# A third seven-product chunk in each wide round, with two weight sums made by adding DMAs

## The reference

```python
h = h + 0.5 * swiglu(rmsnorm(h, ffn1_norm[l]), ffn1_w_in[l], ffn1_w_out[l])   # w_in 2048 x 11264, w_out 5632 x 2048
u = rmsnorm(h, mix_norm[l]) @ w_in_mix[l]
...                                                                            # pooling and gated linear attention
h = h + 0.5 * swiglu(rmsnorm(h, ffn2_norm[l]), ffn2_w_in[l], ffn2_w_out[l])
...                                                                            # sparse attention, stick-breaking attention
```

## Time and profile before

| | before |
|---|---|
| median of 3 runs | 2668.81 us (2668.37 to 2668.97) |
| the profiled execution: time | 2668.85 us |
| the profiled execution: span of the trace | 2667.1 us |
| matmuls | 12038 |
| DMA traffic | 550.9 MB, mean 207 GB/s |

### The profile page before, as it was taken

The page is one execution under the profiler, slowest core; times in us unless marked ns, Lnnn a source line. Parts: engine busy times, 40 slices in busy tenths (PEclk is TensorE's granted clock), DMA queues, the critical chain, the costliest instruction groups (busy, mean ns, idle before and its releaser), DMA issues.

```text
span 2667.1 us, 32619 instructions
## 1 busy us (share of the span) xinstructions
PE 2655.7 (100%) x12038; PEld 2193.6 (82%) x12038; DVE 1926.6 (72%) x2464; ACT 1392.4 (52%) x1836; POOL 58.2 (2%) x64
## 2 busy tenths in 40 slices
PE   9999999999999999999999999999999999999999
PEld 7888888888888788888888888887888888888887
DVE  6888889886645466888888886758555576566566
ACT  6555555454544445555555454555554464675463
POOL 0000000000000000000000000030000000020000
PEclk9999999999999999999999999999999999999999
DMA  9767677677845466666576667755467576546754
GB/s 303 232 198 236 194 231 222 205 222 240 257 144 174 146 219 211 212 225 224 181 246 204 222 213 226 253 186 158 137 186 258 166 237 211 174 143 206 240 181 135
DMA packets 348575, 550.89 MB, mean 207 GB/s; under 512 B 40992, under 2 KB 120096, under 8 KB 347648
## 3 DMA queue, kind: packets, MB, share of 16 engines
q1 hardware_dynamic: 346624, 539.90, 63.4%
q0 software_dynamic: 1648, 8.86, 1.0%
q10 hardware_dynamic: 144, 0.04, 0.0%
HBM read 525.59 MB, written 23.07 MB: 206 GB/s over the span
## 4 chain that ended last, share of the span: by engine, by line
PE 98%; DMA 1%; SPq 0%; DVE 0%; ACT 0%; issue 0%; ACTq 0%; DVEq 0%
PE bank L1467 17%; PE bank L1469 17%; PE bank L1468 17%; PE bank L1536 14%; PE bank L1535 14%; PE bank L1534 14%; DMA raw<-in_ffn_w_in_dram 1%; PE bank L1426 1%; PE bank L1134 0%; PE bank L886 0%; PE bank L870 0%; PE bank L1114 0%; PE bank L568 0%; PE bank L840 0%; SPq L1315 0%
## 5 line engine op out<-in xcount | busy, mean ns | idle before, releaser
L1965 DVE TENSOR_TENSOR wlo<-raw,whi 128x1024 fp32r<-128x1024 f32 (+3 forms) x559 | 641.9, 1158 | 542.8 <-ACT whi L1616 537.8
L1616 ACT CAST whi<-raw 128x1024 fp32r<-128x1024 f32 (+3 forms) x559 | 548.9, 990 | 649.5 <-PE bank L1469 623.8
L1756 ACT CAST whi<-raw 128x1024 fp32r<-128x1024 f32 (+1 forms) x416 | 409.2, 998 | 413.3 <-PE bank L1536 405.8
L2125 DVE TENSOR_TENSOR wlo<-raw,whi 128x1024 fp32r<-128x1024 f32 (+1 forms) x416 | 463.3, 1150 | 67.3 <-ACT whi L1756 64.9
L1467 PE MATMUL bank<-whi,p_hi 128*128 128x512 f32 x1184 | 465.6, 393 | 3.1 <-DVE wlo L1965 3.1
L1469 PE MATMUL bank<-whi,p_lo 128*128 128x512 f32 x1184 | 461.1, 389 | 0.0
L1468 PE MATMUL bank<-wlo,p_hi 128*128 128x512 f32 x1184 | 460.9, 389 | 0.0
L1467 PE MATMUL bank<-whi,q_hi 128*128 128x512 f32 x864 | 340.6, 394 | 0.5 <-DVE wlo L1965 0.5
L1469 PE MATMUL bank<-whi,q_lo 128*128 128x512 f32 x864 | 336.6, 390 | 0.0
L1468 PE MATMUL bank<-wlo,q_hi 128*128 128x512 f32 x864 | 336.3, 389 | 0.0
L1467 PEld LDWEIGHTS bank<-whi,p_hi 128*128 128x128 f32 x1184 | 222.4, 188 | 52.7 <-issue 5.7
(11 more groups left out here) (381 smaller groups left out, 2984.6 us busy)
## 6 DMA issues: line engine op xcount, KB each, us to landing
raw<-in_ffn_w_in_dram SPq DMA_DIRECT2D x704, 256.0 KB, 3.8
raw<-in_ffn_w_out_dram SPq DMA_DIRECT2D x320, 256.0 KB, 4.0
raw<-in_w_in_a_dram SPq DMA_DIRECT2D x192, 256.0 KB, 3.1
raw<-in_w_in_mix_dram SPq DMA_DIRECT2D x128, 256.0 KB, 3.2
raw<-in_w_ple_gate_dram SPq DMA_DIRECT2D x128, 256.0 KB, 3.7
raw<-in_w_in_b_dram SPq DMA_DIRECT2D x128, 256.0 KB, 3.1
raw<-in_w_out_mix_dram SPq DMA_DIRECT2D x64, 256.0 KB, 3.3
raw<-in_w_o_a_dram SPq DMA_DIRECT2D x64, 256.0 KB, 3.7
```

Of the source, the lines that this page charges most:

```text
L1616: act.copy(whi[:, c % SPLIT, 0:n, 0:w], raw[:, c, 0:n, 0:w]).then_inc(hi_done, 1)
L1756: act.copy(whi[:, i % SPLIT, 0:n, :], raw[:, i % CH, 0:n, :]).then_inc(hi_done, 1)
L1965: dve.tensor_tensor(wlo[:, c % SPLIT, 0:n, 0:w], raw[:, c, 0:n, 0:w], whi[:, c % SPLIT, 0:n, 0:w].bitcast(F32), ALU.subtract).then_inc(lo_ ...
L2125: dve.tensor_tensor(wlo[:, i % SPLIT, 0:n, :], raw[:, i % CH, 0:n, :], whi[:, i % SPLIT, 0:n, :].bitcast(F32), ALU.subtract).then_inc(lo_d ...
```

## The change

`SEVEN` becomes (1, 3, 5). The first two weight sums of a chunk are made by a ScalarE copy of two blocks into `w_sums` (`weight_blocks`) and by two DMAs of GpSimd that add the third block, read again from HBM (`add_blocks`). VectorE makes only the other two sums. The order by hand is changed around this, and the buffers of operand sums hold three sets. The DMA descriptor scratch is set to 8192. The core of the diff:

```diff
-SEVEN = (2, 5)
+SEVEN = (1, 3, 5)
...
 SP, load and load_wide, behind the wait for lo_done:
+                        if unit_at(s, wide, i) - CH in summed_units:
+                            sp.wait_ge(t24_sum, summed_units[unit_at(s, wide, i) - CH] + 1)
...
 GpSimd, called for ffn1 after the constants are loaded and for ffn2 after the mixer's:
+            def add_blocks(tag):
...
+                    for i, c in enumerate(SEVEN):
+                        pool.wait_ge(sem("t13_blocks"), seven_number(s, wide, i) + 1)
...
+                        for m in range(2):
+                            pool.dma_start(w_sums[:, m, :], b12, accum_op=ALU.add).then_inc(t13_sum, 16)
...
 ScalarE:
-                for j in range(2):
-                    ins = act.copy(pair_hi[s.hid_pair][:, k * 2 + j, :].rearrange("p (t q n) -> p t q n", t=TT, q=4),
-                                   hidf[:, u, :, j, :, :].rearrange("p q t n -> p t q n"))
-                ins.then_inc(hid_hi, 1)
+                act.copy(pair_hi[s.hid_pair][:, k * 2:k * 2 + 2, :].rearrange("p j (t q n) -> p (j t) q n", t=TT, q=4),
+                         hidf[:, u, :, :, :, :].rearrange("p q j t n -> p (j t) q n")).then_inc(hid_hi, 1)
...
+            def weight_blocks(s, wide, c):
+                q = seven_number(s, wide, SEVEN.index(c))
+                if q:
+                    act.wait_ge(t13_used, q)
+                a_ = 2 * c % CH
+                for n in range(2):
+                    act.wait_ge(landed[a_ + n], (s.r0 + 2 * wide + 2 * c // CH) * 32 + 32)
+                act.copy(w_sums[:, 0:2, :], raw[:, a_:a_ + 2, 0, :]).then_inc(sem("t13_blocks"), 1)
...
             def begin_wide(s, wide, before):
+                weight_blocks(s, wide, SEVEN[0])
                 for i in range(3):
                     wide_hi(s, wide, i)
...
             def wide_round(s, wide):
+                sums_13_hi(s, wide, SEVEN[0])
+                sums_24_hi(s, wide, SEVEN[0])
                 for c in range(2, CH):
                     wide_hi(s, wide, 2 * c)
+                    if c - 1 in SEVEN[1:]:
+                        sums_13_hi(s, wide, c - 1)
+                        sums_24_hi(s, wide, c - 1)
...
                     wide_hi(s, wide, 2 * c + 1)
                     if c in SEVEN:
-                        weight_sums_hi(s, wide, SEVEN.index(c))
-                    if c == 3:
+                        weight_blocks(s, wide, c)
+                    if c == 4:
                         if s.kind == "ffn_out" and wide == 0:
-                            operand_sums_hi(s, 1)
-                        if s.kind == "ffn_in" and wide == 3:
-                            operand_sums_hi(after(s, 2 * wide)[0], 0)
-                    if c == 5:
+                            operand_sums_hi(s, 2)
+                        if s.kind == "ffn_in" and wide in (2, 3) and s.name[-1] != "2":
+                            operand_sums_hi(by_name[s.name.replace("in", "out")], wide - 2)
+                    if c == 6:
                         for s_, k_ in halves_behind(s, wide):
                             hidden_hi(s_, k_, k_ % 2)
...
 VectorE:
             def weight_sums(s, wide, c):
...
-                b12 = raw[:, a_ + 1, 1, :].unsqueeze(1).to_broadcast([P, 2, NB])
-                dve.tensor_tensor(w_sums[:, 0:2, :], raw[:, a_:a_ + 2, 0, :], b12, ALU.add).then_inc(t13_sum, 1)
-                dve.wait_ge(t13_sum, q + 1)
+                dve.wait_ge(t13_sum, 32 * (q + 1))
                 link(dve.tensor_tensor(w_sums[:, 2, :], w_sums[:, 1, :], raw[:, a_, 0, :], ALU.add))
                 dve.tensor_tensor(w_sums[:, 3, :], w_sums[:, 2, :], raw[:, a_, 1, :], ALU.add).then_inc(t24_sum, 1)
...
             begin_wide, after a wide round:
-                    evacuate_wide(before[0], before[2])
+                    evacuate_wide(before[0], before[2], (0,))
+                    weight_sums(s, wide, SEVEN[0])
+                    evacuate_wide(before[0], before[2], (1,))
...
             def wide_round(s, wide):
                 before = ahead_of(s, 2 * wide)
+                weight_sums_lo(s, wide, SEVEN[0])
                 for c in range(2, CH):
+                    if c == CH - 1:
+                        combine_products(s, wide)
+                    wide_lo(s, wide, 2 * c)
+                    wide_lo(s, wide, 2 * c + 1)
+                    if c == 2 and before[2] is not None:
+                        finish_wide(before[0], before[2])
                     if c in SEVEN:
                         weight_sums(s, wide, c)
...
                         weight_sums_lo(s, wide, c)
...
                     if c == 4:
...
+                            operand_sums(s, 2)
+                        if s.kind == "ffn_in" and wide in (2, 3) and s.name[-1] != "2":
+                            operand_sums(by_name[s.name.replace("in", "out")], wide - 2)
                     if c == 5:
+                        if s.kind == "ffn_out" and wide == 0:
+                            operand_sums_lo(s, 2)
...
+                    if c == 6:
                         for s_, k_ in halves_behind(s, wide):
                             hidden_lo(s_, k_, k_ % 2)
...
-    nc = _bacc.Bacc("TRN2", target_bir_lowering=False, num_devices=1)
+    nc = _bacc.Bacc("TRN2", target_bir_lowering=False, num_devices=1, dynamic_dma_scratch_size=8192)
```

More of the change, by code:

```diff
@@ L293, in seven_number @@
         def seven_number(s, wide, i):
-            return 2 * wides.index((s.name, wide)) + i
+            return len(SEVEN) * wides.index((s.name, wide)) + i
         GAIN = dict(ffn1=0, mix=16, ffn2=32, final=48, pool=64, gla=72)
@@ L485, in unit_at @@
             return (s.r0 + 2 * wide) * CH + i
+        summed_units = {unit_at(s, wide, 2 * c + n): seven_number(s, wide, i) for s, _, wide in flat if wide is not None
+                        for i, c in enumerate(SEVEN) for n in range(2)}
         def unit_tiles(i):
@@ L495, in operand_number @@
         def operand_number(s, i):
-            return 6 * (s.name[3] == "2") + (i + 1 if s.kind == "ffn_in" else 3 + 2 * int(s.name[-1]) + i)
+            return 9 * (s.name[3] == "2") + (i + 1 if s.kind == "ffn_in" else 4 + 3 * int(s.name[-1]) + i)
         def sums_done(eng, s, k):
@@ L1374, in _ @@
         def _(pool):
+            def add_blocks(tag):
+                for s, _, wide in flat:
+                    if wide is None or not s.name.startswith(tag):
+                        continue
+                    w, k0, n0 = s.weights
+                    for i, c in enumerate(SEVEN):
+                        pool.wait_ge(sem("t13_blocks"), seven_number(s, wide, i) + 1)
+                        rows = slice(k0 + 2 * c * P, k0 + (2 * c + 1) * P)
+                        b12 = w[rows, 1, n0 + wide * NB:n0 + (wide + 1) * NB] if s.kind == "ffn_in" else w[rows, (2 * wide + 1) * NB:(2 * wide + 2) * NB]
+                        for m in range(2):
+                            pool.dma_start(w_sums[:, m, :], b12, accum_op=ALU.add).then_inc(t13_sum, 16)
             pool.memset(ident, 1.0).then_inc(sem("ident_ones"), 1)
@@ L1887, in second_half @@
                             x_squares(0)
-                        if s.name[-3:] == "in0" and k == 1 and c >= 6:
-                            operand_sums_hi(s, c - 6)
+                        if s.name[-3:] == "in0" and k == 1 and c >= 5:
+                            operand_sums_hi(s, c - 5)
                         if peeled:
@@ L2002, in hidden_lo @@
                 dve.wait_ge(hid_hi, s.hid0 + k + 1)
[L2003 to L2007 removed]
+                hi_, lo_ = (pair[s.hid_pair][:, k * 2:k * 2 + 2, :].rearrange("p j (t q n) -> p (j t) q n", t=TT, q=4)
+                            for pair in (pair_hi, pair_lo))
+                dve.tensor_tensor(lo_, hidf[:, u, :, :, :, :].rearrange("p q j t n -> p (j t) q n"), hi_.bitcast(F32),
+                                  ALU.subtract).then_inc(hid_done, 1)
             def block_lo(s, k):
@@ L2179, in combine_products, with evacuate_wide @@
                 link(dve.tensor_tensor(y_, w_, p7, ALU.add))
-            def evacuate_wide(s, wide):
-                for n in range(2):
+            def evacuate_wide(s, wide, blocks):
+                for n in blocks:
                     dve.wait_ge(chunk_used, unit_at(s, wide, 14 + n) + 1 + USED0)
@@ L2302, in first_half @@
                     if before and before[2] is not None and c == 1:
-                        evacuate_wide(before[0], before[2])
+                        evacuate_wide(before[0], before[2], (0, 1))
                     if before and before[2] is not None and c == 3:
@@ L2338, in round_ @@
                             operand_lo(s, b, u)
-                        if s.name[-3:] == "in0" and k == 1 and c < 6:
+                        if s.name[-3:] == "in0" and k == 1 and c < 7:
                             operand_sums(s, c - 4)
                         if s.name[-3:] == "in0" and k == 1 and c == CH - 1:
-                            for i in range(2):
```

(1 more changed line is left out.)

55 lines of the change are left out of this document (20 added, 35 removed).

## The result

The changed kernel takes **2926.99 us** (median of 4 runs, 2924.7 to 2930.23) against 2668.62 (4 runs, 2668.37 to 2668.97): the ratio is 1.0969 with a 95% interval of 1.0955 to 1.0982, so 258 us slower. The profiled execution took 2927.42 us, with a span of 2925.7. The direction was forecast and the time lies in the range, but the loss is more than twice the 116.6 us of the sum.

The account below looks back on a forecast made before the run. TensorE, busy 2655.7 of 2667.1 us, bounds the kernel. Minus 17.7 for matmuls, plus waits of 27.6 (plain rounds), 85.4 (twelve rounds) and 21.3 (chunk 7): 2668.85 + 116.6 = 2785 us; range 2688 to 2952.

Parts of the forecast that it names:

- the loop and its order: Each chunk by seven: TensorE uses sums, ScalarE copies, GpSimd's DMAs add, VectorE forms sums and low parts, TensorE waits.
- the copy behind the high operand sums: ScalarE, twelve rounds: chunk 5's copy queues behind high operand sums and is done 11.15 us after chunk 3's landing.
- chunk 1's sums: Start of a wide round: copy has half a round of lead; costs nothing until L passes 7 us.
- The forms of the waits: TensorE's waits in chunks 3 and 5 together: 2L - 9.03 us a plain round, 2L - 3.88 in twelve with operand sums.
- L: Time from the end of ScalarE's copy to the landing of both adds; taken as 5.5 us, at least 2.6.
- the eight rounds: Wide 2 and 3 of in0 and in1, both FFNs, among twelve with operand sums in chunk 4: wait 2L - 3.88 us.
- a free addition at 4.0: GpSimd's DMAs: if adding costs nothing, L is 0.8 + 3.2 = 4.0 us, time 2722 us; chance 0.27.
- rival (e): TensorE's clock falls to 1.2 GHz after 7 us gaps: 33 us in twelve rounds, 2818 us; chance 0.08.
- Wide 0 of out0 and out1: Four of the twelve rounds with operand sums: wait 2L - 3.88 us each, and 2.1 us more at chunk 7.
- Chunk 7: VectorE's combinations ahead of the weight split make TensorE wait: 0.55 us in six rounds, 1.2 in eight, 2.1 in four.
- rival (d): Adding DMAs slow, row after row through loaded engines: L of 7 to 9 us, 2863 to 2970 us; chance 0.17.
- (c): The prediction's own case for the adding DMAs: L of 4.5 to 7 us, 2733 to 2863 us; chance 0.36.

Follow-up runs that it names:

- e10: Changed kernel with only chunk 1's first two sums by copy and adding DMAs, chunks 3 and 5 on VectorE, operand sums and low parts reordered: 2659.13 us.
- e1: Changed kernel with the addition taken out of GpSimd's two DMAs, which only write (output not the reference's): 2806.59 us.
- e9: Changed kernel with SP holding four loads of the next round until chunk 5's adds have landed: 2910.3 us.
- e4: Changed kernel without ScalarE's copies and GpSimd's adding DMAs, all weight sums on VectorE: 2711.8 us.
- e6: Changed kernel with its own landing buffer, copy one chunk earlier, descriptor reserve 4096 and operand sums reordered on ScalarE and VectorE: 2766.56 us.
- e0: Changed kernel with only the reserve for GpSimd's DMA descriptors halved to 4096: 2946.07 us.

## Why the prediction was wrong in size

**Right:** the bound; the 17.7 us (78 matmuls fewer; e10 keeps 9.5 of them after its own losses); the loop and its order; the copy behind the high operand sums; chunk 1's sums, but for one round in 26. The forms of the waits hold too: with the measured L of both chunks, 6.6 + 8.6 - 9.03 = 6.2 us against 1.8 + 3.8 measured in a plain round, and 7.0 + 6.6 - 3.88 = 9.7 against 2.2 + 7.2 in the eight rounds (medians). They hold in e1 as well, where only chunk 5 still waits in most rounds: 4.5 + 7.1 - 9.03 = 2.6 against 2.5, and 4.5 + 3.95 - 3.88 = 4.6 against 4.5.

**The step that failed is the size of L.** 5.5 was taken; it is 6.6 to 7.0 in chunk 3 and 6.2 to 8.6 in chunk 5. The step put a free addition at 4.0, and e1 measured 4.5 and 3.95, so the plain part was right. Two terms were too small: the addition (2.1 to 2.7 us by e1, where 1.5 was taken), and the loads that share the DMA engines (2.3 us in chunk 5 of a plain round by e9, for which there was no term of its own; the share of 0.70 in the earlier trace rows is a mean over a round, while in 398.38 to 406.11 it is 0.93). The trace of the kernel before had this: in the round of the earlier trace rows the share is 0.29 in chunk 2, where chunk 3's adds set out in the changed kernel, and 1.00 in chunk 4, where chunk 5's adds are on their way:

```profile
319.28:324.04 4.76, 4.76 (x22) 3.94 (x21) 4.73 (x9) 3.05 (x3) 0.00 (x0) 1.00 0.29 68
...
329.48:334.92 5.44, 5.44 (x25) 4.50 (x24) 4.54 (x8) 4.47 (x8) 0.00 (x0) 1.00 1.00 351
```

In plain rounds, L enters twice, just above the point where it begins to cost: 80.3 us instead of 27.6. The eight rounds cost 72.0 instead of 57.0.

The Trainium skill ("DMA: Bandwidth & Descriptors", section on the anatomy of a GpSimd DMA) gives 2.6 us for 256 KB by its formula (an estimate from that page). Here the DMAs that only write took 3.4 to 3.6 beside the loads, those that add 5.3 to 5.9; the measurement decides.

**The clock, rival (e),** had 0.08 and 33 us; it cost 68.5. The prediction looked for it behind gaps of 7 us in twelve rounds. The rows show it behind waits of 1.93 and 2.81 us as well, so in the plain rounds and in chunk 3 too: 31.0 us lie in the twelve rounds, close to the 33 priced for them, and 36.1 in the fourteen plain ones, for which nothing was. Rival and forecast were no alternatives: the clock came on top. The Trainium skill ("TensorE: Matmul & The Clock Gate", part 1) says that an idle TensorE is gated to 1.2 GHz; the trace agrees, with a pitch of 0.42 us at 0.57.

**Wide 0 of out0 and out1** was given 7.1 us a round for the sums and 2.1 at chunk 7. It cost 50.0 in four rounds: by the pitches TensorE waits 41.1 at the head of chunk 5 for the low operand sums (the 31.7 and 8.7 of the view), which stand on VectorE behind the weight sums and so behind the landing, and another 8.9 at chunk 3's sums. The row of the wait, not only its length, was misread. **Chunk 7** was given 21.3 us, and no wait over 0.6 us stands there; that TensorE's waits and slower pace at chunk 5 gave VectorE the time back is an argument, not shown. **Chunk 1** was given nothing and cost 3.4 us in the first wide round: there VectorE waits 2.19 us for the adding DMAs, ahead of the low parts of units 2 and 3; e4, which has no such DMA, waits 2.2 us in the same places, so most of it is not theirs.

Together: plain rounds +52.7, the eight +15.0, the four +21.5, chunk 7 -21.3, chunk 1 +3.4, clock +68.5, that is 139.8 of the 139.9 us between the sum (116.6) and the 256.5 that the trace holds.

That the time lies in the stated range, and among the times of rival (d), is in part luck: less the clock's 68.5 us it would be 2858, at the upper end of the forecast (c). The L of chunk 3, and of chunk 5 outside the plain rounds, is about (c)'s largest (6.2 to 7.0); only chunk 5 of the plain rounds, with 8.6, has (d)'s.

**What stays open:** why L is 8.5 to 10.1 us in e6 in the rounds where both DMAs were issued at once. The loads are the likely cause (the DMA share is 0.97 over the way shown there, 0.90 over that of after and 0.82 over that of e9), but no run holds them back in e6.

## What to carry to other kernels

Price a new step in a loop between engines by its way under the load of that stage, and by the DMA share of its own few microseconds, not of the round; where it enters twice and stands just above the point from which it costs, give it the upper end. A wait of TensorE can cost more than its length, as the clock can fall behind it (here 68.5 us on top of 205.7). Put slow, free engines where the lead is half a round (chunk 1 here) and keep the short loops on the engine that needs no transfer.

## What was not expected of the hardware

- An adding DMA of 256 KB from HBM into SBUF took 5.3 to 5.9 us to land, the same DMA without the addition 3.4 to 3.6; one of 512 KB that adds, 5.5 to 6.0.
- An earlier issue does not land earlier by as much: in plain rounds L grew from 6.6 us (chunk 3) and 8.6 (chunk 5) to 8.8 and 9.2 when the copy came earlier (e6), and in chunk 5 it fell to 6.3 when the loads were held (e9).
- With a descriptor reserve of 4096 GpSimd's second issue started 0.26 us after the landing of the first DMA in six rounds, 4.6 to 5.0 us after the first issue; in e0's other rounds, and always in the changed kernel with its 8192, it came 0.5 to 0.8 us after it.
- GpSimd's two issues took 1.75 us when the DMAs add, 1.07 when they only write.
- The granted clock fell to its lower level behind a wait of TensorE of 1.93 us, and matmuls started every 0.42 us until 398.2; behind a wait of 2.16 us in another round it stayed at 1.00.
